# Forgetting attention with wide fp32r products of values and probabilities, and the next unit's token tiles beside the last head

## The reference

```python
def forgetting_attention(q, k, v, f_logit, b_f):
    ...
    q = heads(q) * (HEAD_DIM ** -0.5)
    ...
    log_f = jax.nn.log_sigmoid((f_logit + b_f).astype(jnp.float32))
    c = jnp.cumsum(log_f, axis=1).transpose(0, 2, 1)
    def block(i):                       # one block of 128 queries
        s = jnp.einsum('bhqd,bhkd->bhqk', qi, k).astype(jnp.float32)
        s = s + ci[..., None] - c[:, :, None, :]
        s = jnp.where(k_pos[None, :] <= q_pos[:, None], s, -jnp.inf)
        p = jax.nn.softmax(s, axis=-1).astype(v.dtype)
        return jnp.einsum('bhqk,bhkd->bhqd', p, v)
```

## Time and profile before

| | us |
|---|---|
| median of the runs | 1600.95 |
| profiled execution | 1600.94 |
| its span | 1599.2 |
| PE busy | 1572.5 (98%) |
| DVE busy | 744.0 |
| ACT busy | 549.6 |
| POOL busy | 512.6 |

### The profile page before, as it was taken

One profiled execution on the slowest core, in us unless ns is written; L12 is line 12 of the kernel. 1 busy time (PEld: TensorE's weight loads), 2 busy tenths in 40 slices (PEclk: granted clock), 3 DMA queues, 4 the chain that ended last, 5 costly groups with the idle time before them and its releaser, 6 DMA issues.

```text
span 1599.2 us, 20117 instructions
## 1 busy us (share of the span) xinstructions
PE 1572.5 (98%) x7720; PEld 1310.0 (82%) x7720; DVE 744.0 (47%) x962; ACT 549.6 (34%) x821; POOL 512.6 (32%) x450
## 2 busy tenths in 40 slices
PE   7999999999999999999999999999999999999998
PEld 7878888888888888888887777888888888888886
DVE  4342665447543333322265988744445433333224
ACT  4323333223542222222265566322226422223121
POOL 2880001310188158377110710683003870000000
PEclk9999999999999999999999999999999999999999
DMA  6542122222445345344231121353232453342231
GB/s 200 159 157 79 53 79 54 80 79 79 149 142 157 105 125 151 116 146 158 79 93 53 53 80 52 114 158 111 93 105 82 137 150 92 92 118 81 103 105 52
DMA packets 189297, 170.90 MB, mean 107 GB/s; under 512 B 20657, under 2 KB 161969, under 8 KB 189233
## 3 DMA queue, kind: packets, MB, share of 16 engines
q1 hardware_dynamic: 181168, 144.84, 29.8%
q0 software_dynamic: 8064, 25.20, 5.0%
HBM read 167.91 MB, written 2.10 MB: 106 GB/s over the span
## 4 chain that ended last, share of the span: by engine, by line
PE 92%; DVE 4%; ACT 2%; POOL 1%; issue 1%; DMA 0%; DVEq 0%; SPq 0%; ACTq 0%
PE bank L1784 28%; PE bank L1786 28%; PE bank L1785 28%; PE bank L2012 1%; PE bank L1992 1%; DVE w_lo L1204 1%; PE bank L1910 1%; PE bank L2063 1%; POOL inv_rms L704 1%; PE bank L2001 1%; PE bank L1951 0%; PE bank L2032 0%; POOL sq_x L703 0%; PE bank L2073 0%; DMA x_in<-in_x 0%
## 5 line engine op out<-in xcount | busy, mean ns | idle before, releaser
L1784 PE MATMUL bank<-h_hi,w_hi 128*128 128x512 f32 (+1 forms) x1504 | 566.2, 376 | 5.3 <-DVE w_lo L1216 1.8
L1785 PE MATMUL bank<-h_lo,w_hi 128*128 128x512 f32 (+1 forms) x1504 | 559.3, 372 | 0.0
L1786 PE MATMUL bank<-h_hi,w_lo 128*128 128x512 f32 (+1 forms) x1504 | 559.3, 372 | 0.0
L1204 DVE TENSOR_TENSOR w_lo<-raw,w_hi 128x2048 fp32r<-128x2048 f32 (+1 forms) x146 | 303.0, 2076 | 310.0 <-ACT w_hi L839 309.8
L1784 PEld LDWEIGHTS bank<-h_hi,w_hi 128*128 128x128 f32 x1504 | 284.2, 189 | 65.3 <-issue 10.1
L1786 PEld LDWEIGHTS bank<-h_hi,w_lo 128*128 128x128 f32 x1504 | 284.1, 189 | 49.5
L1785 PEld LDWEIGHTS bank<-h_lo,w_hi 128*128 128x128 f32 x1504 | 284.4, 189 | 46.0
L839 ACT CAST w_hi<-raw 128x2048 fp32r<-128x2048 f32 (+1 forms) x145 | 244.0, 1682 | 220.3 <-PE bank L1786 220.3
L759 POOL TENSOR_SCALAR mod_raw<-mod_raw,c_silu 128x512 f32<-128x512 f32 x96 | 173.0, 1802 | 44.1 <-DMA mod_raw<-in_mod_w 40.1
L762 POOL TENSOR_TENSOR mod_acc<-mod_acc,mod_raw 128x512 f32<-128x512 f32 x96 | 152.2, 1585 | 8.2
L1784 PE MATMUL bank<-w_hi,act_hi 128*128 128x512 f32 x352 | 137.7, 391 | 0.0
(11 more groups left out here) (358 smaller groups left out, 1817.4 us busy)
## 6 DMA issues: line engine op xcount, KB each, us to landing
raw<-in_w_in SPq DMA_DIRECT2D x102, 512.0 KB, 4.6
mod_raw<-in_mod_w POOLq DMA_DIRECT2D x96, 256.0 KB, 3.2
raw<-in_w_ffn_in SPq DMA_DIRECT2D x44, 512.0 KB, 4.6
raw<-in_w_gate SPq DMA_DIRECT2D x22, 512.0 KB, 4.0
raw<-in_w_up SPq DMA_DIRECT2D x22, 512.0 KB, 5.3
raw<-in_w_down SPq DMA_DIRECT2D x20, 512.0 KB, 4.2
raw<-in_w_ffn_out SPq DMA_DIRECT2D x20, 512.0 KB, 4.1
raw<-in_w_out SPq DMA_DIRECT2D x8, 512.0 KB, 4.2
```

Of the source, the lines that this page charges most:

```text
L1204: ins = dve.tensor_tensor(w_lo[s][:, cols], raw[s][:, cols], w_hi[s][:, cols].bitcast(F32), ALU.subtract)
L1784: pe.matmul(o, st_hi, mv_hi, start=first, stop=False)
L1785: pe.matmul(o, st_hi, mv_lo, start=False, stop=False)
L1786: return pe.matmul(o, st_lo, mv_hi, start=False, stop=last)
```

## The change

1. The product of values and probabilities is taken once per head instead of once per task. The transposed probabilities of all four query blocks are kept in `pt_hi` and `pt_lo` (fp32r), laid out so that all queries of key block j that are at or behind it lie side by side (`pt_row`). Per head there are 4 key blocks times 3 passes, with 512, 384, 256 and 128 columns; the stationary operand is now the value block.
2. The split is made by two engines: ACT casts bank 6 into `pt_hi` (`pt_hi_part`), DVE subtracts into `pt_lo` in the place of its copy to `prob_t`. Values are split too: ACT makes `v_hi`, DVE `v_lo`, once per head.
3. In the two steps behind the last task PE makes token tiles 0 and 1 of unit `n_vs`; tiles 2 and 3 come behind the `w_sp` transposes, still before `mod_columns(0)`. The second unit comes behind it. The loop over chunks is written out.
4. The load of `b_sp` leaves the group of small loads at the start and is issued by SP behind the `vs` stream and a wait for the last `head_out`; DVE waits for it before the gating stage.

```diff
+        v_lo = at("v_lo", 80, [P, NT, D], F32R)
-        prob_t = at("prob_t", A + 68, [P, 2, TOK])
+        pt_hi = at("pt_hi", A + 68, [P, NT * PT_STEP + TOK - P], F32R)
+        pt_lo = at("pt_lo", A + 80, [P, NT * PT_STEP + TOK - P], F32R)
+        v_hi = at("v_hi", M + 16.5, [P, 2, NT, P], F32R)
...
+        def pt_blocks(t, i):
+            return t[:, P * i:P * i + PT_STEP * (i + 1)].rearrange("p (j n) -> p j n", n=PT_STEP)[:, :, 0:P]
+        def pt_row(t, j):
+            return t[:, PT_STEP * j + P * j:PT_STEP * j + TOK]
...
             stream_t(n_vs, w_in, VS_COL)
+            sp.wait_ge(head_out, HEADS)
+            sp.dma_start(b_sp[:], a["b_spatial"][0].partition_broadcast(P)).then_inc(b_sp_in, 16)
...
+            def pt_hi_part(s):
+                h, i = ATT_TASKS[s]
+                act.wait_ge(pt_ready, s + 1)
+                wait(act, pv_done, h)
+                act.copy(pt_blocks(pt_hi, i), bank[:, 6, 0:P * (i + 1)].rearrange("p (j n) -> p j n", n=P)).then_inc(pt_hi_done, 1)
...
                 act.activation(prob[:, s % 2, 0:w], prob[:, s % 2, 0:w], ACT.Exp, bias=neg_max[:, s % 2:s % 2 + 1],
                                accum_out=row_sum[:, s % 2:s % 2 + 1]).then_inc(prob_ready, 1)
+                if s > 0:
+                    pt_hi_part(s - 1)
                 if i == 0:
+                    wait(act, pv_done, h - 1)
+                    act.copy(v_hi[:, h % 2, :, :], v_att[:, :, P * h:P * h + P]).then_inc(v_hi_done, 1)
...
-                    dve.wait_ge(pv_done, s - 2)
+                    dve.wait_ge(pv_done, ATT_TASKS[s - 3][0] + 1)
...
-                    dve.tensor_copy(prob_t[:, b, 0:w], bank[:, 6, 0:w]).then_inc(pt_copied, 1)
+                    dve.wait_ge(pt_hi_done, s)
+                    dve.tensor_tensor(pt_blocks(pt_lo, i1), bank[:, 6, 0:P * (i1 + 1)].rearrange("p (j n) -> p j n", n=P),
+                                      pt_blocks(pt_hi, i1).bitcast(F32), ALU.subtract).then_inc(pt_lo_done, 1)
                 if s < len(ATT_TASKS) and i in (1, 2):
                     split(n_g + h + 1, part=i - 1)
+                if s < len(ATT_TASKS) and i == NT - 1:
+                    dve.wait_ge(v_hi_done, h + 1)
+                    dve.tensor_tensor(v_lo[:, :, P * h:P * h + P], v_att[:, :, P * h:P * h + P], v_hi[:, h % 2, :, :].bitcast(F32),
+                                      ALU.subtract).then_inc(v_lo_done, 1)
...
+                else:
+                    t = s - len(ATT_TASKS)
+                    token_unit(n_vs, h_hi, h_lo, 0, True, False, STILL, tiles=range(t, t + 1))
...
-                    for j in range(i + 1):
-                        ins = pe.matmul(bank[:, 7, P * i:P * i + P], v_att[:, j, P * h:P * h + P],
-                                        prob_t[:, b, P * j:P * j + P], start=(j == 0), stop=(j == i))
+                if s >= 2 and ATT_TASKS[s - 2][1] == NT - 1:
+                    h = ATT_TASKS[s - 2][0]
+                    pe.wait_ge(v_lo_done, h + 1)
+                    pe.wait_ge(pt_lo_done, s - 1)
+                    wait(pe, head_out, h)
+                    for j in range(NT):
+                        o, vs = bank[:, 7, P * j:TOK], slice(P * h, P * h + P)
+                        pe.matmul(o, v_hi[:, h % 2, j, :], pt_row(pt_hi, j), start=j == 0, stop=False, skip_group_check=True)
+                        pe.matmul(o, v_hi[:, h % 2, j, :], pt_row(pt_lo, j), start=False, stop=False, skip_group_check=True)
+                        ins = pe.matmul(o, v_lo[:, j, vs], pt_row(pt_hi, j), start=False, stop=j == NT - 1, skip_group_check=True)
...
+            token_unit(n_vs, h_hi, h_lo, 0, True, False, STILL, tiles=range(2, NT))
             pe.wait_ge(head_out, HEADS)
             mod_columns(0)
-            chunks(n_vs, h_hi, h_lo)
+            token_unit(n_vs + 1, h_hi, h_lo, 4, False, True, STILL)
+            for j in range(2):
+                token_unit(n_vs + j, h_hi, h_lo, 4 * j, j == 0, j == 1, chunk_pace(1))
```

More of the change, by code:

```diff
@@ L56 @@
 CONV_K, SHORT_K = 4, 3
+PT_STEP = 384
 PAD = CONV_K
@@ L346, in build @@
         c_spread, c_kept = sems("c_spread", "c_kept")
-        pt_ready, pt_copied, pv_done, head_out, gated_b = sems("pt_ready", "pt_copied", "pv_done", "head_out", "gated_b")
+        pt_ready, pt_hi_done, pt_lo_done, pv_done, head_out, gated_b = sems(
+            "pt_ready", "pt_hi_done", "pt_lo_done", "pv_done", "head_out", "gated_b")
+        v_hi_done, v_lo_done, b_sp_in = sems("v_hi_done", "v_lo_done", "b_sp_in")
         wsp_tr, wsp_done, v_normed, sgu_ready = sems("wsp_tr", "wsp_done", "v_normed", "sgu_ready")
@@ L517, in build @@
         POST_UNIT = [n_out + 3, n_dn + 11, n_out2 + 3, n_dn2 + 11]
-        SMALL, SMALL_2 = 10, 14
+        SMALL, SMALL_2 = 9, 14
         wf_hi, wf_lo = ktiles(wf_both, KD, 40)[:, :, 0:8], ktiles(wf_both, KD, 40)[:, :, 32:40]
@@ L1003, in _ @@
                     take(n_va + 1, t, v_att[:, t, 512 * c:512 * c + 512], chunk_pace(c))
+            def pt_hi_part(s):
[3 more added lines that the diff above has]
+                act.copy(pt_blocks(pt_hi, i), bank[:, 6, 0:P * (i + 1)].rearrange("p (j n) -> p j n", n=P)).then_inc(pt_hi_done, 1)
+            for t in range(NT):
+                wait_emptied(act, n_va + 3, t)
             for s, (h, i) in enumerate(ATT_TASKS):
@@ L1016, in _ @@
                     take(n, 0, gates[:, 2 * h, :], STILL, ACT.Tanh, 0.5)
+            pt_hi_part(len(ATT_TASKS) - 1)
             take(n_vs - 1, 1, gates[:, 2 * KD - 1, :], STILL, ACT.Tanh, 0.5)
@@ L1441, in _ @@
             dve.wait_ge(gated_b, KD)
+            dve.wait_ge(b_sp_in, 16)
             for f in range(KD):
@@ L1848, in f_pairs, with token_unit @@
                             feature_tile(n0 + j, f, pair_pace(i))
-            def token_unit(n, x_hi, x_lo, k0, first, last, pace, width=512):
+            def token_unit(n, x_hi, x_lo, k0, first, last, pace, width=512, tiles=range(NT)):
                 u = UNITS[n]
@@ L1855, in token_unit @@
                 wait(pe, lo_done, n + 1 + pace.by(pace.units))
-                for t in range(NT):
+                for t in tiles:
                     ts = slice(P * t, P * t + P)
@@ L1864, in token_unit @@
                         ins.then_inc(acc_full, 1)
-                if not last:
+                if not last and t == NT - 1:
                     ins.then_inc(mid_used, 1)
[L1868 to L1872, removed]
             def out_chunks(n0, x_hi, x_lo, there, c, xn, gate=None):
@@ L1998, in _ @@
                     pe.wait_ge(prob_scaled, s)
-                    wait(pe, pt_copied, s - 1)
+                    wait(pe, pt_lo_done, s - 1)
                     for j in range(i + 1):
```

5 lines of the change are left out of this document (1 added, 4 removed).

## The result

| | before | after |
|---|---|---|
| median of the runs, us | 1601.2 (20 runs) | 1603.55 (20 runs, 1602.72 to 1607.99) |
| span of the profiled execution, us | 1599.2 | 1602.2 |
| PE busy, us | 1572.5 | 1572.1 |
| granted clock, mean | 0.998 | 0.996 |

The ratio after to before is 1.0017, with a 95% interval of 1.0010 to 1.0023: slower by 2.35 us in the medians. The interval lies above 1, so the loss is real, and 0.17% is inside the 0.2% that the prediction called no change. The two profiled spans differ by 3.0 us.

The account below looks back on a forecast made before the run. PE, busy 1572.5 of 1599.2 us, was taken as the bound. From 1600.94 us, -3.2 (values) + 0.5 (late `pt_lo`) - 0.9 (old waits) + 0.15 (switches) + 3.9 (stall) + 2.0 (clock) gave 1603.4 us; range 1600.0 to 1606.5.

Parts of the forecast that it names:

- Values' product, -3.2: In each head, wider fp32r passes take 1.83 us instead of 2.23, saving 3.2 us over eight heads (2.3 to 4.2).
- Late `pt_lo`, +0.5: In the heads, transposes of task (h, 3) may wait for DVE's later `pt_lo`: 0.5 us for all heads (0 to 2.5).
- The rival in which DVE's chain binds: In each head, transposes of (h, 3) wait for `pt_lo`; seven heads lose 3.5 us, giving 1606.4 us; chance 0.20.
- Old waits, -0.9: Behind the last head, token tiles 0 and 1 fill PE's waits for DVE's copies, saving 0.9 us.
- Switches, +0.15: Behind the last head, three more switches between float32 and fp32r cost 0.15 us, at 0.05 each.
- Stall, +3.9: Behind the one-column products, PE waits for DVE's `w_lo` of unit `n_vs + 1`: 3.9 us (3.75 to 4.5).
- Clock, +2.0: TensorE's clock falls to half in the stall behind the one-column products, losing 2.0 us (0 to 3.4).
- The rival in which it holds (1601.4): The stall behind the one-column products is there but TensorE's clock does not fall: 1601.4 us; chance 0.25.
- Load of `b_sp`, 0: Moving this load from the first loads to behind the `vs` stream changes nothing either way.

Follow-up runs that it names:

- the run with the longer chain: Fastest version (changed kernel, one-column products ahead of token tiles 2 and 3) with DVE's head-output copy written twice in seven heads: 1602.16 us.
- the run with the old values: Kernel before with its old values' products, plus tiles 0 and 1 beside the last head and one-column products ahead of tiles 2 and 3: 1600.68 us.
- the run with the gap filled: Changed kernel plus 16 unread fp32r products of 512 columns between the one-column products and the second unit: 1601.88 us.
- the maskings: Changed kernel with DVE's two maskings of the spatial weights ahead of its copy of the modulation columns: 1602.91 us.
- the version without tiles: Changed kernel without token tiles beside the last head, so new values' products with before's order behind it: 1604.02 us.

## Why the prediction was right, and where it wasn't

Point by point, with what was measured:

- **Values' product, -3.2.** The passes take 1.87 us for 1.83, but a head is shorter by 0.28 and not by 0.40. The old form took 2.22, so the gross saving is 0.35. The other 0.07, in the head shown, is 0.04 in the scores of 384 columns that now follow the product (0.75 for 0.71 until the full passes start) and 0.04 in the 48 full passes (11.23 for 11.19), none with a wait. In the trace it comes to 2.30 up to the last transposes and 0.15 in the last head's product (1.85 for 2.00), 2.45 in all; 2.7 to 2.9 in the medians. This was the largest error of size, inside its bounds of 2.3 to 4.2 but near their low end. (At the 0.45 ns per column that the prediction states, its lower figure of 1.70 would be 1.73; nothing hangs on it.)
- **Late `pt_lo`, +0.5.** No wait in the heads, and 0.17 behind the last one. The instants were right (P + 1.49 for 1.55, P + 10.59 for 10.72, PE at P + 10.91 for 10.88), and the slack is 0.17 where 0 to 0.1 was counted. The rival in which DVE's chain binds was 0.17 us away, and the run with the longer chain shows what it would have cost.
- **Old waits, -0.9.** 0.88 in the run with the old values. In the changed kernel 0.17 of the new wait is left, so 0.75. What the prediction missed is that its own delay of DVE by 2.03 us also holds behind the last head, where no full passes hide it. With the new values' products and no tiles the waits are 4.2 and not 0.93 us. It made nearly no difference to the sum, because the tiles, put there for the short waits, cover the long ones too. That was luck.
- **Switches, +0.15.** Not told apart: the tail's sum below closes without them.
- **Stall, +3.9.** A wait of 3.65 us for `w_lo`, by the steps that were counted: copy and maskings 1.3, then `w_lo` 2.2, and 0.1 until PE starts.
- **Clock, +2.0.** It fell, and cost 2.22 us by the spacing of the passes and 1.7 by the run with the gap filled. The rival in which it holds (1601.4) is that run: 1601.88. The Trainium skill, in "TensorE: Matmul & The Clock Gate", section "Why this matters for your kernels", warns that idle gaps of a few microseconds between bursts of matmuls halve the clock. The wait of 3.65 us agrees with it. The wait of 2.58 us, and those of 2.73 and 1.45 us with four transposes between, are shorter than the gap that the page names, and the clock fell there too.
- **Load of `b_sp`, 0.** It lands 6.0 us after its issue (307.3), and its reader starts at 353.1. The attention's first scores start at 154.68 to 155.57 us in the seven traces with the load moved, and at 155.27 to 155.64 in the three without, so leaving the first loads changed nothing that can be told from chance.

Laid along PE's path, the two traces compare as follows (the marks are the first scores of the attention, the three transposes behind the last head, the first and the 13th pass of unit `n_vs + 1`, and PE's last pass):

| stretch | before, us | after, us | difference |
|---|---|---|---|
| start to first scores | 155.27 | 155.45 | +0.18 |
| first scores to the three transposes | 132.72 | 130.42 | -2.30 |
| transposes to unit `n_vs + 1` | 17.47 | 20.21 | +2.74 |
| its first 12 passes | 2.73 | 4.95 | +2.22 |
| the rest of the run | 1282.93 | 1283.13 | +0.20 |

The third line is 3.65 for the stall, -0.75 for the old waits and -0.15 for the last product. So the change itself is worth +2.66 us in the traces, and 0.38 of the 3.04 lies where both kernels execute the same instructions, but for the load of `b_sp`. The forecast of +2.45 was this near because an error of 0.75 in the values' product and one of 0.5 in the late `pt_lo` had opposite signs and partly cancelled.

What stays open: the 0.3 to 0.5 us by which the medians and the traces disagree on the values' products. Single traces differ by more than that in stretches that the change does not touch: the first scores start up to 0.96 us apart in the ten traces. The 95% intervals of the ratios are some 1.4 us wide to either side, so medians that differ by less, such as those of the maskings, show no effect by themselves.

## What to carry to other kernels

Before a block of work is moved ahead of a small operation, look who waits behind that operation: here sixteen records of 1.8 us released DVE's copy, and with it the next unit's operands, and their place was worth 5.9 us. An engine that is off the path inside a loop can be on it behind the loop. Here DVE fell 2 us behind PE in every head at no cost, and behind the last head, in the version without tiles, the split cost 2.5 us by it and by the cast in series. Small products can also be the cover of a dependency (1.1 us here); when they are merged into one block behind it, the wait they hid shows up, so a saving has to be counted with its new neighbours. Where the clock falls, a wait costs more than its length: here 3.65 us of it cost 2.2 more and 2.58 us cost 3.0 more, and shortening it gave little as long as the clock still fell.

## What the runs showed of the hardware

- Work that nobody reads made the kernel faster twice: 16 products by 1.7 us, with every filled run faster than every unfilled one, and 19 by 1.3 us, with a small overlap of the runs. Both times the granted clock held at 1.00 where it had fallen to half.
- With a shorter gap (2.58 for 3.65 us) the clock fell and came back at nearly the same instants (303.7 and 303.8, 310.7 and 310.8), not the same time after work stopped or resumed: 13 slow passes for 11. It fell 1.4 us after the last one-column product, where at the end of the run before it had held for 2.4 us after the last matmul.
- fp32r products of 128 columns come 0.06 to 0.12 us apart in the values' product, of 256 columns 0.12, of 384 columns 0.18, of 512 columns 0.23; the first of 512 behind a float32 transpose takes 0.31 (193.17 to 193.48).
